# Latent attention: the exponential of a step one slot later on ScalarE; the rotary tables made under the first down projection

## What is computed

```python
def partial_rope(x, positions):                    # only used in layer 1
    ang = positions[..., None] * freqs
    cos, sin = jnp.cos(ang), jnp.sin(ang)
    return concat([x1 * cos - x2 * sin, x2 * cos + x1 * sin, rest])

def dsa_attention(q, k_lat, q_idx, k_idx, w_idx):  # layer 1, per block of 128 queries
    score = einsum('bqh,bqhs->bqs', wb, relu(einsum('bqhd,bsd->bqhs', qib, kif)))
    top_val, top_idx = lax.top_k(where(visible, score, -inf), 256)
    k_sel = k_lat[top_idx]
    p = softmax(einsum('bqhd,bqkd->bqhk', qb, k_sel) * scale)
    return einsum('bqhk,bqkc->bqhc', p, k_sel[..., DSA_ROPE:])

def conv_ffn(x, w_up, conv_w, conv_b, w_down):
    gate, up = split(x @ w_up)
    return (gelu(conv(gate)) * up) @ w_down
```

## Time and profile before

| | |
|---|---|
| time, median of 3 runs | 3183.16 us (3181.98 to 3184.33) |
| the profiled execution, its own time | 3195.31 us |
| its span from first to last instruction | 3193.5 us |
| TensorE busy | 2943.2 us, 92% |
| VectorE, ScalarE, GpSimd busy | 57%, 32%, 45% |
| mean granted TensorE clock | 0.975 |
| attention stage of layer 1 | about 2008 to 2392 us |
| first down projection (dn0), TensorE | about 1132 to 1370 us |

### The profile page before, as it was taken

The page is one execution under the profiler, slowest core; times in us unless marked ns, Lnnn a source line. Parts: engine busy times, 40 slices in busy tenths (PEclk is TensorE's granted clock), DMA queues, the critical chain, the costliest instruction groups (busy, mean ns, idle before and its releaser), DMA issues.

```text
span 3193.5 us, 45888 instructions
## 1 busy us (share of the span) xinstructions
PE 2943.2 (92%) x17190; PEld 1524.1 (48%) x17472; DVE 1805.8 (57%) x2540; ACT 1026.3 (32%) x1671; POOL 1442.3 (45%) x721
## 2 busy tenths in 40 slices
PE   5899997999999999959799999888889999999998
PEld 3556665444444444434344444555654444444443
DVE  7687556474444414154699999566655744444042
ACT  3556667112222200014653334445540221222000
POOL 3577221654344378644017776200006533443785
PEclk8999999999999999979899999999999999999999
DMA  4222321411111132211003222011103111111322
GB/s 145 65 57 63 74 57 27 165 54 53 53 52 46 53 106 93 86 60 53 13 6 126 105 105 90 32 51 39 39 26 120 53 53 53 52 46 53 112 99 99
DMA packets 96516, 218.24 MB, mean 68 GB/s; under 512 B 41328, under 2 KB 41456, under 8 KB 96416
## 3 DMA queue, kind: packets, MB, share of 16 engines
q1 hardware_dynamic: 54048, 195.74, 18.0%
q10 hardware_dynamic: 42368, 21.11, 2.8%
HBM read 176.92 MB, written 23.12 MB: 63 GB/s over the span
## 4 chain that ended last, share of the span: by engine, by line
PE 39%; DVE 8%; ACT 5%; issue 3%; POOL 1%; DVEq 0%; DMA 0%; ACTq 0%; POOLq 0%; SPq 0%
PE ps L301 24%; PE ps L312 8%; PE ps L1865 3%; DVE prob L1942 2%; DVE score L1588 1%; DVE pt_lo L1934 1%; PE ps L336 1%; ACT strip_w L1534 1%; ACT strip_w L1449 1%; ACT pt_hi L1913 1%; PE ps L1901 1%; PE ps L1681 1%; ACT prob L1923 1%; PE ps L1880 1%; POOL w_hi L271 0%
## 5 line engine op out<-in xcount | busy, mean ns | idle before, releaser
L271 POOL TENSOR_TENSOR w_hi<-w_stage,ones 128x1024 bf16<-128x1024 f32 x227 | 454.8, 2004 | 940.2 <-PE ps L301 540.3
L301 PE MATMUL ps<-xt_hi,w_hi 128*128 128x512 bf16 x1888 | 565.4, 380 | 33.9 <-ACT strip_f L1450 29.7
L301 PE MATMUL ps<-xt_lo,w_hi 128*128 128x512 bf16 x1889 | 566.0, 380 | 1.6
L301 PE MATMUL ps<-xt_hi,w_lo 128*128 128x512 bf16 x1880 | 563.6, 380 | 2.1
L274 POOL TENSOR_TENSOR w_lo<-w_stage,w_hi 128x1024 bf16<-128x1024 f32 x227 | 520.4, 2292 | 17.8
L301 PEld LDWEIGHTS ps<-xt_hi,w_hi 128*128 128x128 bf16 x1920 | 187.9, 98 | 259.6 <-issue 29.8
L301 PEld LDWEIGHTS ps<-xt_hi,w_lo 128*128 128x128 bf16 x1920 | 188.3, 98 | 227.7 <-issue 2.1
L301 PEld LDWEIGHTS ps<-xt_lo,w_hi 128*128 128x128 bf16 x1920 | 188.2, 98 | 227.4 <-issue 1.6
L1219 DVE SCALAR_TENSOR_TENSOR x_res<-x_res,ps 128x1024 f32<-128x1024 f32 x32 | 38.9, 1216 | 417.8 <-PE ps L312 417.8
L1347 DVE TENSOR_SCALAR conv_up<-gate_up,conv_w_up 128x1024 f32<-128x1024 f32 x44 | 78.4, 1782 | 283.2 <-ACT gate_up L1328 282.7
L312 PE MATMUL ps<-w_hi,hid_hi 128*128 128x512 bf16 x689 | 206.2, 379 | 5.6 <-DVE x_res L1219 4.0
(11 more groups left out here) (230 smaller groups left out, 5746.2 us busy)
## 6 DMA issues: line engine op xcount, KB each, us to landing
w_stage<-in_l_up SPq DMA_DIRECT2D x88, 512.0 KB, 3.3
w_stage<-in_l_down SPq DMA_DIRECT2D x88, 512.0 KB, 3.3
w_stage<-in_l_o SPq DMA_DIRECT2D x32, 512.0 KB, 3.9
w_stage<-in_l_q SPq DMA_DIRECT2D x32, 512.0 KB, 5.4
q_split<-q_out SPq DMA_DIRECT2D x32, 512.0 KB, 2.6
q_now<-q_split SPq DMA_DIRECT2D x16, 1024.0 KB, 4.9
w_stage<-in_l_qkv SPq DMA_DIRECT2D x24, 512.0 KB, 3.5
k_twice<-nk_hi ACTq DMA_DIRECT2D x32, 128.0 KB, 2.9
```

The source lines that it names most:

```text
L271: pool.tensor_tensor(w_hi[slot][:, 0:cols], w_stage[slot][:, 0:cols], ones[:, 0:1].to_broadcast([P, cols]), ALU.mult).then_inc(w_cast[slot ...
L301: mm = pe.matmul(ps[:, bank + h, :], w, a[:, k, h * HALF:(h + 1) * HALF], start=(first and k == k0 and m == 0), stop=(last and k == k1 - 1 ...
```

## The change

The exponential on ScalarE is taken with lag 1: in slot s, behind the high parts of step s-3, stands the exponential of step s-1 in place of that of step s. The rotary tables leave the opening and the heads phase: loads, angles, sines, finish and stores now stand at the start of dn0 on SyncE, VectorE and ScalarE, in the room of `xt_hi` and `xt_lo`, which are free there. The waits for the stored tables go with them. In the opening ScalarE copies the q and k halves out, issues both groups of q and k copies, and then takes the value halves.

```diff
@@ latent_scalar
-                if kind:
-                    t, i, hh = slot, query_block(slot), slot // 8
+                p, t = steps_behind(act, pair, slot, kind, prev, 1)
+                if t is not None:
+                    i, hh = query_block(t), t // 8
                     n = span[i]
-                    act.wait_ge(t_nm, STEPS * pair + t + 1)
+                    act.wait_ge(t_nm, STEPS * p + t + 1)
                     act.activation(prob7[t % 4][:, 0:n], prob7[t % 4][:, 0:n], ACT.Exp, scale=DSA_SCALE,
...
@@ start_sync
-            sp.dma_start(pos_i[:, :], t_in["positions"]).then_inc(s_pos, 16)
-            sp.dma_start(rope_rows[:, :], t_in["rope_rows"]).then_inc(s_pos, 16)
@@ start_vector
-            rotary_angles(dve, 0)
@@ rooms
-        scratch = Room(room.at)
+        scratch = Room(xt_at)
+        rope_rows = scratch("rope_rows", [P, 4], F32)
@@ pair_scalar
-                    if prev is None and at == 0:
-                        act.wait_ge(s_tabst, 64)
@@ heads_scalar
-            rotary_sines(act, 0)
-            rotary_store(act, 0)
-            proj_evac_hi(act, 0, 0)
-            proj_evac_hi(act, 1, 0)
-            rotary_sines(act, 1)
             act.preload_act_table_set("sigmoid_and_others")
-            for e in range(2, 6):
+            for e in range(4):
                 proj_evac_hi(act, e, 0)
             for hh in range(2):
                 make_current_qk(act, hh, 0)
+            for e in range(4, 6):
+                proj_evac_hi(act, e, 0)
             for hh in range(2):
                 make_current_v(act, hh, 0)
-            rotary_store(act, 1)
@@ heads_vector
...
+            for e in range(6):
+                proj_evac_lo(dve, e, 0)
...
+        def rotary_scalar(act):
+            for t in range(2):
+                rotary_sines(act, t)
+                rotary_store(act, t)
+            act.wait_ge(s_tabst, 64)
+
+        def rotary_vector(dve):
+            for t in range(2):
+                rotary_angles(dve, t)
+                rotary_finish(dve, t)
@@ back_and_norm, sync_program
                 if after:
                     sp.wait_ge(after["hidden_lo"], FT)
+                if rotary:
+                    rotary_sync(sp)
                 sp.dma_start(g_rows[:, :], names[0]).then_inc(s_gb, 16)
...
+                if rotary:
+                    sp.wait_ge(s_tabst, 64)
@@ back_and_norm, scalar_program and vector_program, ahead of deviation(0) and accumulate(0)
+                if rotary:
+                    rotary_scalar(act)
...
+                if rotary:
+                    rotary_vector(dve)
```

More of the change, by code:

```diff
@@ L200, in program @@
         w_lo = [wroom(f"w_lo{s}", [P, KT * P], BF16) for s in range(SLOTS)]
+        xt_at = wroom.at
         xt_hi = wroom("xt_hi", [P, KT, SEQ], BF16)
@@ L375, in program @@
         xt_f = room("xt_f", [P, KT, SEQ], F32)
-        rope_rows = room("rope_rows", [P, 4], F32)
         wf_f = room("wf_f", [P, KT, 8], F32)
@@ L969, in heads_sync @@
             load_first(sp, feed_o0)
-            sp.wait_ge(s_tabst, 64)
         def heads_gpsimd(pool):
@@ L1019, in heads_vector @@
         def heads_vector(dve):
-            rotary_finish(dve, 0)
-            proj_evac_lo(dve, 0, 0)
-            proj_evac_lo(dve, 1, 0)
-            rotary_angles(dve, 1)
-            proj_evac_lo(dve, 2, 0)
-            proj_evac_lo(dve, 3, 0)
-            rotary_finish(dve, 1)
-            proj_evac_lo(dve, 4, 0)
-            proj_evac_lo(dve, 5, 0)
+            for e in range(6):
+                proj_evac_lo(dve, e, 0)
             for b in range(4):
@@ L1033, in heads_vector, with rotary_sync @@
             all_pairs(dve, pair_vector)
+        def rotary_sync(sp):
+            sp.dma_start(pos_i[:, :], t_in["positions"]).then_inc(s_pos, 16)
+            sp.dma_start(rope_rows[:, :], t_in["rope_rows"]).then_inc(s_pos, 16)
+        def rotary_scalar(act):
[7 more added lines that the diff above has]
+                rotary_finish(dve, t)
         opening = phase(start_sync, start_gpsimd, start_tensor, start_scalar, start_vector)
@@ L1041, in back_and_norm @@
         def back_and_norm(tag, feed, tiles, act_hi, act_lo, names, free_at, bank_of, next_feed, early, load_x=None,
-                          final=None, after=None, started=None):
+                          final=None, after=None, started=None, rotary=False):
             room = Room(free_at)
@@ L1396, in program @@
             back_and_norm("dn0", feed_down0, FT, hid_hi, hid_lo, (t_in["l0_ln2_g"], t_in["l0_ln2_b"]),
-                          after_hid, (0, 4, 2, 6), feed_small, early_small(feed_small), after=up0_sems))
+                          after_hid, (0, 4, 2, 6), feed_small, early_small(feed_small), after=up0_sems, rotary=True))
         clear_sems()
```

## The result

The changed kernel takes **3093.5 us** (median of 4 runs, 3091.9 to 3095.6) against 3183.7 us before (4 runs, 3182.0 to 3187.0): ratio 0.9716, 95% interval 0.9700 to 0.9731, so 2.8% or 90 us less. The forecast was 3084.4, or 98.8 us less, with a range of 3068 to 3116. The sign and the range came out right, and the gain was forecast 9 us too high.

The account below looks back on a forecast made before the run. TensorE, busy 92%, was taken as the bound, so only its idle places or waits pay. From 3195.3 us, less 72.8 (attention), 26 (opening) and 0 (down projection): 3096.5, or 3084.4 us on the median scale, range 3068 to 3116.

Parts of the forecast that it names:

- The two places named: Hole near 54 to 76 us in the opening, and layer 1 attention, 2008 to 2392 us, with compute engines partly idle.
- Part 1, attention: Latent attention: exponential behind the high parts of two steps earlier cuts a ScalarE-VectorE loop; TensorE becomes the limit; gain 72.8 us.
- 16 x (24.15 - 19.6): Latent attention gain: 16 heads, each going from 24.15 to 19.6 us, 72.8 us in all.
- Part 2, opening: Opening: without rotary tables on ScalarE the first sigmoid comes at 60.6 instead of 85.53; 26 us gained, ends 21 and 28.
- Removing 512 KB of positions ahead of the first weights: Opening: the weights' earlier arrival is worth at most TensorE's 0.53 us wait for the first split; counted as nothing.
- my steps: Opening: count from TensorE's start at 22.20 through projection halves, copies and value halves to the first sigmoid at 60.6 us.
- the mark of a wrong part 2: Opening: a first sigmoid later than 65 us would show the forecast for moving the tables wrong.
- the slow end of my own range: Whole kernel: about 3100 us, from 60 gained in attention, 21 in the opening, a few us lost in the down projection.
- Part 3, down projection: First down projection: the moved table work hides in VectorE's 104.78 us idle time, and splits keep TensorE's pace; cost 0.
- The rival with splits that starve TensorE: Down projection: 21 table operations slow GpSimd pieces to 5.9 us against 5.18; TensorE waits 4 us; 3088 us, chance 0.10.
- Another loop in attention: Latent attention: high parts, low parts and next transposes through two banks close a loop; half the gain, 3121 us, chance 0.13.
- The slower case: Latent attention: exponential and high part in series ahead of the transposes make slots 4.15 us; 3302 us, chance 0.04.

Follow-up runs that it names:

- experiments 1 and 2: First: kernel before with only the late latent exponential, ratio 0.9781, 3116.3 us. Second: changed kernel with the exponential back, only the tables moved, ratio 0.9942, 3166.8 us.
- Experiments 3 and 4: Changed kernel, first: GpSimd's splits wait for VectorE's low parts, 3091.5 us; second: unread positions loaded ahead of the weights again, 3093.2 us.
- experiment 8: Changed kernel plus 14 unread two-input VectorE operations behind the rotary tables under the first down projection: 3099.3 us, ratio 0.9724.
- experiment 6: Changed kernel with the third product of the latent scores (low query by high key) left out: ratio 0.9571.
- experiment 7: Kernel before, with VectorE's mask and maximum taken ahead of the low parts in latent attention: 3223.3 us, ratio 1.0115.
- split_again: Repeat run of the changed kernel with GpSimd's first weight splits held until VectorE has written the input's low parts: 3091.4 us, ratio 0.9714.

## Why the prediction was right, and where it was not

**What bounds the kernel.** Right. The two places named were the two that paid, and experiments 1 and 2 give them 70 and 18 us.

**Part 1, attention.** The mechanism was right in every step: waits for the maximum fell from 190.9 to 14.5 us and those for pt_lo to 4.7, ScalarE idles ahead of high parts, and the transposes wait for exponentials for well under a microsecond in the whole stage, against a gain of 68. The account of TensorE's work was good too. From first to last exponential there are 127 steps, or 15.9 heads, so a head now takes 312.1 / 15.9 = 19.7 us against my 19.6. Mis-sized was the other side of the difference, "16 x (24.15 - 19.6)". I read 24.15 us from one pair of widest exponentials, but over the stage it was 380.0 / 15.9 = 23.9. And it is 15.9 such heads, not 16. So 67.9 us by the trace, 70 (65 to 74) by the runs of experiment 1, for my 72.8.

**Part 2, opening.** This is the step that failed: "Removing 512 KB of positions ahead of the first weights is worth at most the 0.53 us that TensorE waits for the first split; taken as nothing." At the first projection it was worth minus 5 us. I bounded it by TensorE's wait for the split, thus as a transfer that comes sooner or not, and did not ask what the split itself would meet when it came sooner. The row on which I counted, a first projection at 22.20, held only with the splits at 16.5. Experiments 3 and 4 give most of it back by two unlike edits, and then the first sigmoid is at 61.2 and 61.4, where my steps said 60.6. The rest of the steps up to the sigmoid were right: 0.9 us of waiting for k_ext and the clock at 1.00. The sigmoid at 65.1 is just over the 65 that I had named as the mark of a wrong part 2. In device time the moved tables gave 18 us (14 to 23) for my 26, and the collision accounts for a part of the difference at most: without it the kernel is 0 to 4 us faster by the medians, and the intervals overlap. I had carried the sigmoid's gain over into the device time one for one, with 1 us on top for the clock, and no run shows this step. Where the rest went stays open. (A slip besides: the slow end of my own range, "about 3100", adds up to 3102 and those few us more.)

**Part 3, down projection.** Right: cost 0, 110.06 us in both profiles. The reason held too, that the pace of the splits stays under TensorE's 5.18 us, but more narrowly than my 4.84: beside the mix of one-input and two-input operations a piece took 5.14 us in the mean. The rival with splits that starve TensorE had its head start nearly right (3.7 us forecast, some 3.2 in experiment 8) and its price for a piece beside two-input operations (5.9 forecast, 5.90 measured). It was wrong in charging this price for all 21 operations, of which 13 have one input.

**The rule on the shared ports.** In the prediction I said that the trace agreed less as to GpSimd. That held for the one-input operations of the earlier trace rows. Beside two-input operations both sides pay: a half of a split goes from 1.90 and 2.12 to 2.87 and 2.98, and VectorE's operation from 1.2 to 2.95 us. In 5.90 us there are then one piece (4.0 alone) and two operations (2.4 alone): 6.4 us of work, nearly one after the other. By the Trainium skill (SBUF — State Buffer, section Who interferes with whom) the loser fully blocks for a whole instruction; for these operations the trace agrees but for some 0.5 us in 6.4. I had used that section for the down projection, where the tables cost nothing, and did not apply it to the opening, where the splits made the first projection 5 us late.

**The other rivals.** Another loop in attention did not close: experiment 6 takes a further 48 us out of the stage (46 us by the runs), where TensorE's matmuls wait for pt_lo for 8.2 us. A loop of the kind feared does exist one edit away, as experiment 7 shows. The slower case had no sign of it.

**What stays open.** The two profiles differ by some 12 us outside the two places. Since the profile before is that much above its own median, and experiments 1 and 2 add up, I take this as scatter. The marks say where it lies: 5.2 us between the first sigmoid and the output projection of layer 0, 2.8 from there to the index phase, 0.8 from there to attention and 3.9 behind it. In the first of these stretches the thirteen profiles range over 11 us (469.8 to 480.5), whichever opening they have. Why it varies was not tried.

## What to carry to other kernels

In a pipeline over several engines, look for an operation in an in-order queue that stands ahead of one that does not need it; then move the one whose reader is farthest off, and check for the moved one's own reader in the same slot. Before relying on an engine's share as the next limit, take some of its work away and see whether the time follows. When a change takes a transfer away, ask what its arrival had held back: a start that comes sooner may fall on a neighbour that slows it, as the splits and the low parts did here. And follow an earlier mark to the end of its phase before counting it as time gained.

## What the hardware showed beyond expectation

- Five low parts on VectorE took 13.02 us beside splits that began at 13.5, 7.65 beside splits that began at 16.5, and about 6 without (1.2 each). Held back by 6 us, GpSimd had its first piece ready 4.8 us later (21.46 + 2.12 against 15.76 + 2.99), and yet the projections began 3.5 us sooner (23.64 for 27.17).
- Single runs of one program scatter by 4 to 11 us (the changed kernel 3091.9 to 3095.6, split_again 3088.9 to 3099.7), more than two of the differences studied here. The first sigmoid was steadier: 63.7 to 65.7 us in the five profiles with the changed opening, 61.2 to 62.0 in the three with the collision avoided.
